# First products on one block's tokens, ahead of the other block's transposes, in six stages of a two-model fp32 kernel

## The reference, cut to what matters

```python
x = layer_norm(ALPHA_2 * x + 0.5 * swiglu(x, ffn1_gate[l], ffn1_up[l], ffn1_down[l]), ln_g[l, 0], ln_b[l, 0])
h = x @ w_in[l]
u = h[..., :D_POOL]
q, f_raw, v, g = jnp.split(h[..., D_POOL:], 4, axis=-1)
y_pool = multiscale_pool(u, pool_w[l], pool_scale[l])
o = hgrn2_recurrence(q, f_raw, v, lb_all[l])
y_hgrn = head_rms_norm(o, hgrn_norm_g[l]) * jax.nn.silu(g)
x = layer_norm(ALPHA_2 * x + concatenate([y_pool, y_hgrn]) @ w_out[l], ln_g[l, 1], ln_b[l, 1])
x = layer_norm(ALPHA_2 * x + 0.5 * swiglu(x, ffn2_gate[l], ffn2_up[l], ffn2_down[l]), ln_g[l, 2], ln_b[l, 2])
```

## Time and profile before

| | |
|---|---|
| time, median of 3 runs | 2320.6 us (2320.22 to 2322.26) |
| profiled execution: span, first to last instruction | 2323.1 us, no other time of it is given |
| PE busy | 2166.1 us, 93% |
| DVE busy | 1142.2 us, 49% |
| ACT busy | 784.0 us, 34% |
| mean granted clock of PE | 0.975 of full |
| DMA over the span | mean 268 GB/s |

### The profile page before, as it was taken

One profiled execution on the slowest core, in us unless ns is written; L12 is line 12 of the kernel. 1 busy time (PEld: TensorE's weight loads), 2 busy tenths in 40 slices (PEclk: granted clock), 3 DMA queues, 4 the chain that ended last, 5 costly groups with the idle time before them and its releaser, 6 DMA issues.

```text
span 2323.1 us, 30109 instructions
## 1 busy us (share of the span) xinstructions
PE 2166.1 (93%) x12126; PEld 1528.0 (66%) x12126; DVE 1142.2 (49%) x1786; ACT 784.0 (34%) x1299; POOL 61.5 (3%) x62
## 2 busy tenths in 40 slices
...
GB/s 289 145 175 379 421 421 421 417 421 420 413 246 73 76 363 420 420 421 415 420 420 421 295 209 168 199 128 127 181 200 200 154 208 166 193 96 159 167 208 46
DMA packets 231542, 622.66 MB, mean 268 GB/s; under 512 B 15456, under 2 KB 166944, under 8 KB 182112
## 3 DMA queue, kind: packets, MB, share of 16 engines
...
HBM read 619.51 MB, written 1.05 MB: 267 GB/s over the span
## 4 chain that ended last, share of the span: by engine, by line
PE 41%; DMA 6%; DVE 4%; ACT 2%; issue 1%; POOL 0%; SPq 0%; DVEq 0%; ACTq 0%
PE bank L1517 14%; PE bank L1505 10%; PE bank L1518 7%; PE bank L228 6%; PE bank L1345 3%; DMA arena<-in_moe_w_up 1%; DMA ring<-in_moe_w_up 1%; DMA ring<-in_ffn_gate 1%; DMA w_parts<-in_moe_w_up 1%; DMA x_tok<-in_moe_w_up 1%; DVE w_low L439 1%; PE bank L1673 1%; ACT w_high L432 1%; DVE x_tok L687 0%; DVE x_tok L676 0%
## 5 line engine op out<-in xcount | busy, mean ns | idle before, releaser
L439 DVE TENSOR_TENSOR w_low<-ring,w_high 128x1024 fp32r<-128x1024 f32 x364 | 441.1, 1225 | 271.7 <-ACT w_high L432 271.7
L1517 PE MATMUL bank<-xT_parts,w_high 128*128 128x512 f32 x1408 | 496.2, 395 | 6.0 <-DVE xT_parts L504 6.0
L432 ACT ACTIVATE w_high<-ring 128x1024 fp32r<-128x1024 f32 x364 | 377.1, 1053 | 218.0 <-PE bank L1518 184.6
L1518 PE MATMUL bank<-xT_parts,w_low 128*128 128x256 f32 x1408 | 394.5, 280 | 0.0
L1345 PE MATMUL bank<-ring,arena 128*64 128x512 f32 x1344 | 339.0, 594 | 17.3 <-DMA w_parts<-in_moe_w_gate 5.3
L1517 PEld LDWEIGHTS bank<-xT_parts,w_high 128*128 128x128 f32 x1408 | 264.0, 188 | 69.0 <-DVE xT_parts L504 6.9
L1345 PE MATMUL bank<-w_parts,arena 128*64 128x512 f32 x768 | 263.8, 609 | 13.4 <-DMA w_parts<-in_moe_w_up 6.7
L1518 PEld LDWEIGHTS bank<-xT_parts,w_low 128*128 128x128 f32 x1408 | 265.8, 189 | 3.1
L1345 PEld LDWEIGHTS bank<-ring,arena 128*64 128x64 f32 x1344 | 110.1, 137 | 230.5 <-issue 221.9
L1453 DVE SCALAR_TENSOR_TENSOR arena<-arena,bank 128x512 f32<-128x512 f32 x32 | 23.9, 747 | 434.1 <-PE bank L1345 434.1
L228 PE MATMUL bank<-w_high,xT_parts 128*128 128x256 f32 x1152 | 222.9, 290 | 10.4 <-DVE w_low L439 8.8
(11 more groups left out here) (284 smaller groups left out, 2934.4 us busy)
## 6 DMA issues: line engine op xcount, KB each, us to landing
...
```

The costliest lines, as they stand in the source:

```text
L432: e.activation(hi, src, ACT.Copy).then_inc(*S.high.tell(key))
L439: e.tensor_tensor(lo, src, hi.bitcast(F32), ALU.subtract).then_inc(*S.low.tell(key))
L1517: e.matmul(pairs(bank[:, :]), hi[:, j, :], k.x_parts[:, :, j, :], start=j == 0, stop=False)
L1518: ins = e.matmul(bank[:, 0:T], lo[:, j, :], k.xh[:, j, :], start=False, stop=j == KT - 1)
```

## The change

Seven edits, of which the first five are one design:

1. In an FFN the first two tiles of gate and of up are made together and token-major, block by block (`first_block_pe`, 24 matmuls of 256 columns, into banks 0 to 3): turn block 0, gate of block 0, turn block 1, up of block 0, gate of block 1, transposes of block 0's hidden tiles, up of block 1, gate of tile 2, transposes of block 1's hidden tiles. ACT applies SiLU straight from the bank, DVE multiplies, and PE turns the hidden values.
2. The four parts gate 0, gate 1, up 0, up 1 are split ahead of the stage. The two of up have buffers of their own, one in the arena, one over `mixT`; so has hgrn's chunk 1.
3. In hgrn the order of the chunks becomes 0, 1, 4, 5, 2, 3 and PE makes chunk 0 of block 0 between the two blocks' transposes. ACT and DVE split both chunks 0 and 1 ahead of the layer norm's last part.
4. The fillers become `BUSY_AHEAD`: four ahead of block 0's transposes in ffn 0, none elsewhere in the second model.
5. DVE makes both `x_low` of block 0 ahead of the centring of block 1. In front of ffn 1 and 3 it splits the two parts of up between the scaling and the `x_low` of block 1; in front of ffn 0 it splits gate 1 ahead of `x_low` of block 0 and the two parts of up behind the scaling.
6. `norm_centre_dve` is cut in two functions, with the same instructions.
7. The od stage of the first model gets DVE's new order too: the split of its chunk 0's second part goes between scaling and `x_low` of block 1.

The hunks shown are, in this order: the constants, the new function, `ffn_pe`, `ffn_act`, `hgrn_pe`, `act_program`, `first_block_dve`, `dve_program`.

```diff
-IN2_ORDER = (4, 5, 2, 3, 0, 1, 6, 7, 8, 9)
+IN2_ORDER = (0, 1, 4, 5, 2, 3, 6, 7, 8, 9)
...
+BUSY_AHEAD = {"mixer": 0, "experts": 4, "ffn": 0}
...
+def first_block_pe(e, k, i, name, n, tb):
+    S = k.S
+    keys, views = first_parts(k, i, name)
+    bank = k.banks.open(e, (tb,) if name == "gate" else (2 + tb,), ("ffn", i, name + " sum", tb))
+    if tb == 0:
+        e.wait_ge(*S.low[keys[1]])
+    if name == "gate":
+        x_ready(e, k, n, tb)
+    parts = []
+    for c, (hi, lo) in enumerate(views):
+        parts += block_products(k, tb, hi, lo, c * (KT // 2))
+    ins = mm(e, bank[:, 0:T], parts)
+    ins.then_inc(*(S.product.tell(keys[0]) if tb == 0 else S.used.tell(keys[1])))
...
-    for f in range(FT):
+    transpose_block_pe(e, k, n, 0, BUSY_AHEAD[after])
+    first_block_pe(e, k, i, "gate", n, 0)
+    transpose_block_pe(e, k, n, 1)
+    first_block_pe(e, k, i, "up", n, 0)
+    first_block_pe(e, k, i, "gate", n, 1)
+    first_hidden_pe(e, k, i, 0)
+    first_block_pe(e, k, i, "up", n, 1)
+    for f in range(2, FT):
...
+            if f == 2 and name == "gate":
+                first_hidden_pe(e, k, i, 1)
...
-    S, n = k.S, 4
-    for f in range(FT):
+    S, n = k.S, 8
+    for tb in range(NB):
+        e.wait_ge(*first_done(S, i, "gate", tb))
+        e.activation(k.ffn_gate[:, tb, :], k.banks["ffn", i, "gate sum", tb][:, 0:T], ACT.Silu).then_inc(*S.act_out.tell(("ffn", i, "gate sum", tb)))
+    ffn_fill(e, k, i, 4, 8, split_act)
...
-    project_pe(e, k, inp(4), fresh=n)
-    for c in (5, 2, 3, 0, 1):
+    first = IN2_ORDER[0:2]
+    transpose_block_pe(e, k, n, 0, BUSY_AHEAD["ffn"])
+    for tb in range(NB):
+        for i, c in enumerate(first):
+            bank = k.banks.open(e, A_BANKS, inp(c)) if tb == 0 else k.banks[inp(c)]
+            project_block_pe(e, k, inp(c), bank, tb, n if i == 0 else None)
+            if tb == 0 and i == 0:
+                transpose_block_pe(e, k, n, 1)
+    for c in IN2_ORDER[2:6]:
         project_pe(e, k, inp(c))
...
-            split_chunk(e, k, ("in2", layer, IN2_ORDER[0]), split_act)
+            for c in IN2_ORDER[0:2]:
+                split_chunk(e, k, ("in2", layer, c), split_act)
             split_x_act(e, k, n + 1)
             hgrn_act(e, k, layer)
-            ffn_fill(e, k, i + 1, 0, 2, split_act)
+            ffn_fill(e, k, i + 1, 0, 4, split_act)
             split_x_act(e, k, n + 2)
-            ffn_fill(e, k, i + 1, 2, 4, split_act)
...
+def first_block_dve(e, k, n):
+    x_low_dve(e, k, n, 0, 0)
+    x_low_dve(e, k, n, 0, 1)
     norm_centre_dve(e, k, n, 1)
-    x_low_dve(e, k, n, 0, 0)
     norm_scale_dve(e, k, n, 1)
...
-        norm_after_experts_dve(e, k, k.main[1], 3)
-        x_low_rest_dve(e, k, 3)
-        ffn_fill(e, k, 0, 1, 4, split_dve)
+        norm_after_experts_dve(e, k, k.main[1], 3, (k.ffn_order[0][1:2], k.ffn_order[0][2:4]))
```

More of the change, by code:

```diff
@@ L316, in split_parts @@
         for f in range(FT + FFN_LAG):
-            own += [("ffn", i, "gate", f), ("ffn", i, "up", f)] if f < FT else []
+            if f == 0:
+                own += [("ffn", i, name, part) for name in ("gate", "up") for part in range(2)]
+            own += [("ffn", i, "gate", f), ("ffn", i, "up", f)] if 2 <= f < FT else []
             own += [("ffn", i, "down", f - FFN_LAG)] if f >= FFN_LAG else []
@@ L1487, in ffn_fill, with first_parts, first_hidden_pe, hidden_low @@
         split(e, k, key)
-def ffn_pe(e, k, i, n):
+def first_parts(k, i, name):
+    keys = [("ffn", i, name, part) for part in range(2)]
+    return keys, [split_views(k, key)[1:] for key in keys]
+def first_block_pe(e, k, i, name, n, tb):
+    S = k.S
+    keys, views = first_parts(k, i, name)
[9 more added lines that the diff above has]
+    ins.then_inc(*(S.product.tell(keys[0]) if tb == 0 else S.used.tell(keys[1])))
+def first_hidden_pe(e, k, i, tb):
+    S, key = k.S, ("ffn", i, "turned", 0)
+    if tb == 0:
+        k.banks.open(e, B_BANKS, key)
+    view = pairs(k.banks[key][:, :])
+    e.wait_ge(*S.dve_out["ffn", i, "up sum", tb])
+    for j in range(2):
+        ins = e.transpose(view[:, j, block(tb)], k.ffn_gate[:, tb, block(j)], k.ident)
+    ins.then_inc(*S.product.tell(("ffn", i, "turned", tb)))
+def hidden_low(S, i, f):
+    return S.dve_out["ffn", i, "turned", 0] if f < 2 else S.ffn_low[i, f]
+def first_done(S, i, name, tb):
+    return S.product["ffn", i, name, 0] if tb == 0 else S.used["ffn", i, name, 1]
+def ffn_pe(e, k, i, n, after):
     S = k.S
@@ L1513, in ffn_pe @@
             e.wait_ge(*S.low[key])
-            if f == 0 and name == "gate":
-                x_ready(e, k, n, 1)
             for j in range(KT):
```

159 lines of the change are left out of this document (96 added, 63 removed).

## The result

The changed kernel takes 2341.6 us (median of 4 runs, 2338.4 to 2343.6) against 2321.4 before (4 runs): a ratio of 1.0076, 95% interval 1.0064 to 1.0089, so 15 to 21 us slower. Run again beside the experiments it gave 1.0076 again (1.0063 to 1.0090). I had forecast slower with a chance of 0.79, but 2331.2 us and a range up to 2337: the sign holds, the size doesn't.

A forecast was written before the change was run, and what follows sets the result against it. TensorE was taken as busiest, stage starts mattering through its first useful product. Parts summed to +4.6 us, the clock added +6.0: +10.6 on the profiled 2323.1, giving 2331.2 us on the median of 2320.6; range 2323 to 2337.

The forecast's parts named there:

- Parts 1 and 2: Stage starts and hgrn chunk order: ffn 0 +2.9, ffn 1 and 3 -1.4 each, ffn 2 -1.0, hgrn +0.9, +6.1 us.
- Part 4: PE's clock without most fillers: falls of 1.5 us at five gaps over 3 us, 1.5 taken back at od: +6.0 us.
- The wait of 4 us in ffn 0: In ffn 0 PE waits 4 us for up's splits, since ACT's order is unchanged; the stage was forecast +2.9 us.
- stands for most of 17 us: In hgrn 1 PE, done with chunk 3 at E+40.2 (E: previous stage finished), idles until the first decayed product, E+57.9.
- Part 3: In od, DVE makes the split of chunk 0's second part earlier, for which PE waited 2.59 us: -1.5 us.
- rival (c): Ffn 0 is worse and level stages start at half clock, up to 2 us more each: 2335 us; chance 0.17.
- rival (b): In both hgrn stages the forget chain is covered: -3.3 and -7.3 instead of +0.9 and +6.1, 2313.6 us; chance 0.08.
- (a): The clock holds in PE's new gaps: 2325.2 us, or 2323.7 if od's fall goes too; chance 0.23.
- (d): The change does not reach the path; answered no, as the instruction order moves on three engines; no chance given.

The follow-up runs named there:

- combined run: Changed kernel with hgrn stages as before, ACT's order in ffn 0 mended and half-size fillers in the FFN gaps, against the kernel before: 0.9968, 2319.7 us.
- filler run: Changed kernel with fillers in the gaps of the stage starts (half the first number) and of the hgrn level stages, against the kernel before: 1.0010, 2327.3 us.

## Why the prediction was right in sign and wrong in size

*Parts 1 and 2, the waits: right.* The run with fillers in all gaps is the changed kernel at nearly full clock, so it tests these parts nearly without Part 4. Forecast, and that run less before: ffn 0 +2.9, +3.7; hgrn 0 +0.9, +0.5; ffn 1 -1.4, -1.1; ffn 2 -1.0, -1.5; hgrn 1 +6.1, +5.8; ffn 3 -1.4, -1.1. The sum is +6.1 forecast and +6.2 measured; single stages are off by up to 0.8, and that they cancel is luck. (The kernel before had falls itself, one in hgrn 0 and one in hgrn 1 behind its wait of 4.03, shown below; without the first, as in the combined run's 118.8, hgrn 0 is +1.7.) The wait of 4 us in ffn 0 was 4.17. PE "stands for most of 17 us" was 7.6 + 7.2 and the rest diagonal products.

*Part 3, od: right.* Part 3 forecast -1.5, and Part 4 took back another 1.5 there for the fall of the earlier trace rows: -3.0 together, -2.6 measured. The wait of 2.59 shrank to 0.46, and the products behind it ran at the full step.

*Part 4, the clock: this is the step that failed.* It said "take 1.5 for the five gaps over 3 us, nothing for those of 2.0": 7.5 us in the six stages. Measured: 13.1. The missing 5.6 us have three sources. The price of a fall: I took 1.5 from one row behind a short wait with fillers ahead of it. The 24 products behind the five gaps lost 2.1 and 2.1 in ffn 0, 1.4 in hgrn 0, 2.4 in ffn 2 and 1.6 in hgrn 1 (their times above less 2.88), and by the filler run these gaps cost 9.8 instead of 7.5. The count: the level stages stand in no term of the sum. They paid 1.8 in hgrn 0 and 1.1 in hgrn 1 (3.2 and 2.7 of the filler run, less the 1.4 and 1.6 of the starts); the 16 pool products there take 5.61 and 5.19 instead of 3.62. This stood in rival (c), "up to 2 us more each", as an unlikely addition, when the forecast itself had put waits of 6 and 17 us there, longer than any wait of these stages in the trace of before. The last 0.4 are ffn 1 and ffn 3, put at nothing: the products in ffn 1 lost 1.5, but most of that only took the place of a wait for `up`, 0.93 in ffn 3, where the clock held. With 13.1 in place of 7.5 and the measured -2.6 of od the forecast is 2337.2 us, a ratio of 1.0072, inside the measured interval.

The evidence was in the trace of before. The windows behind the six starts, in the order ffn 0, hgrn 0, ffn 1, ffn 2, hgrn 1, ffn 3:

```profile
1308.70:1312.70 4.00, 4.00 (x23) 3.55 (x24) 4.00 (x5) 1.92 (x3) 0.00 (x0) 1.00 1.01 326
1500.50:1504.50 4.00, 4.00 (x21) 4.00 (x22) 2.36 (x2) 0.94 (x1) 0.00 (x0) 0.58 0.66 230
1620.20:1624.20 4.00, 4.00 (x23) 3.49 (x24) 3.56 (x4) 1.87 (x3) 0.00 (x0) 1.00 0.99 305
1812.50:1816.50 4.00, 4.00 (x23) 3.49 (x24) 3.57 (x4) 1.87 (x3) 0.00 (x0) 1.00 0.91 290
2004.80:2008.80 4.00, 4.00 (x33) 4.00 (x34) 2.36 (x2) 1.01 (x2) 0.00 (x0) 1.00 0.73 227
2130.50:2134.50 4.00, 4.00 (x23) 3.52 (x24) 3.56 (x4) 1.91 (x3) 0.00 (x0) 1.00 0.97 298
```

Only one of six starts with four fillers and a wait of 1.50 had a fall. I had argued from that one that the trace bears the rule out only in part ("although four fillers stood ahead of it"). Five starts at full clock say more for the fillers, and the run without them confirms it with 14.6 us. One more fall stood in these stages, behind the wait of 4.03 in hgrn 1; rival (b) counts it at 1.5. The granted clock there was 0.50:

```profile
2039.80:2043.10 3.30, 3.30 (x18) 3.30 (x17) 3.03 (x6) 0.47 (x1) 0.00 (x0) 0.50 0.94 290
```

So the Trainium skill's rule ("Perfetto Trace Analysis", Matmul Optimizations: matmuls back to back in batches, since the engine scales with its use) weighed more here than I gave it; the runs agree with it, at 13.1 us for the change and 14.6 for the old fillers.

*Rivals.* (a), the clock holds, is what the filler runs made true: 1.0010 is 2322.9 us, forecast 2325.2. (b), the forget chain is covered, is wrong by the chain's 29.0 us. (c) was the nearest case: it named the level stages, with up to 4 us where 2.9 were measured, but kept 1.5 for each gap. (d) was no case.
